# Who scales the probabilities in the mixers' attention heads: VectorE or ScalarE

## The chip, the cores and the metric

The kernel runs on one core of a Trainium2 chip. Its engines are named as in the profile: PE (TensorE, matrix products and transposes), DVE (VectorE), ACT (ScalarE), POOL (GpSimd) and SP (SyncE, which issues the loads). Each has its own queue, carries it out in order and waits for the others by semaphores. The metric is the device time of one execution in microseconds (us), lower is better.

## The reference, cut to what matters

Two transformer blocks run on 256 tokens of width 1024. The second block has two layers. Each begins with a hybrid mixer: a gated delta rule (6 heads), a "forgetting" attention (6 heads) and a pooling branch, whose outputs are concatenated and multiplied by `w_out`. A dense MLP or a mixture of experts follows. The attention is causal, so of the 256x256 scores of a head the block of the first 128 queries has 128 keys, and that of the second has 256:

```python
s = jnp.einsum('bhqd,bhkd->bhqk', q[:, :, lo:hi], k[:, :, :hi]).astype(F32) * scale
s = s + c[:, :, lo:hi, None] - c[:, :, None, :hi]
s = jnp.where(k_pos <= q_pos, s, -jnp.inf)
p = jax.nn.softmax(s, axis=-1).astype(dt)
outs.append(jnp.einsum('bhqk,bhkd->bhqd', p, v[:, :, :hi]))
```

The delta rule needs the inverse of a unit triangular matrix (`triangular_solve` in the reference). The kernel builds it by doubling blocks, in seven levels of which each needs the one before.

## The kernel before, in words

All is float32. A matrix product with weights is done as three products of split numbers: ACT copies a half of a weight tile of 128x2048 into its rounded part (`high`, L1402), DVE subtracts to get the rest (`low`, L1881), PE multiplies (L532 to L534). Three raw tiles (`RING`) and two split ones (`SPLIT`) are in the chip's memory at a time; a split tile is filled again once PE has finished with it.

The order on each engine is written out by hand, once for each engine, in the same steps. In the mixer of layer `l` the six attention heads are interleaved with the levels of the inverse. Step `s` has on each engine:

- PE (`attention`, L627): the scores of head `s`; the transposes of the probabilities of head `s-1` (L646), which wait for `probs`; at odd `s` from 3 the outputs of two heads (L666), which wait for `pt_copied`; then level `s+1` of the inverse (`between_heads`, L1046): twelve products L988, then L997 and L1003 twice. At `s` = 6 there is no level left: `first_chunk` (L1015, `vn0`) stands there, and at `s` = 7 `first_state` (L1041, then L1015 for `o0`), which waits until `vn0` is read.
- DVE (`attention`, L1988): `reciprocal` of the sums of head `s-1` (L1995), the two multiplications by it (L1999, `probs`), the scores of head `s` out of their bank with scale and mask (L2013), their negated row maxima (L2018), then for the inverse `level_mask` (L2354) and the updates (L2405). At `s` = 6 `low(2)` (L1881) stands in the place of the level.
- ACT (`attention`, L1463): first `ahead(s)`, which is the level's copies (`inverse_level`: L1660 `picked` and L1453 `invp`, twice) and at `s` = 6 `high(2)`, four copies of half a weight tile each (L1402); then the exponentials of head `s` (L1459) and the copy of the transposed probabilities of head `s-1` (L1474, `pt_copied`). After step 6 ACT copies out `vn0`, the state and `o0` (L1453).

`PR` holds the scores and then the probabilities of three heads, `RDEN` the reciprocals. The first block's heads (`attention(0, AH)` and `attention(AH, XH)`) use the same functions with `until_now` false.

Of the kernel before, what the change touches and what calls it, by code (L numbers as in the profile page):

```python
# [7 lines left out]
ACT = mybir.ActivationFunctionType  # L8
# [5 lines left out]
TT = S // P  # L14
# [123 lines left out]
def program(nc, A, out, points, stop):  # L138
    ctx = ExitStack()
    with ctx:  # L140
        def sb(name, shape, dt=F32):
            return ctx.enter_context(nc.sbuf_tensor(name, shape, dt))
# [15 lines left out]
        PR = sb("probs", [P, 3, TT, S])  # L158
# [9 lines left out]
        DEN = sb("den", [P, 3, TT])  # L168
        RDEN = sb("rden", [P, 3, TT])
# [110 lines left out]
        def chunk_head(s):  # L280
            return s % 2, s // 2
# [34 lines left out]
        def col(name, i=0):  # L316
            return COL[:, COLS[name] + i:COLS[name] + i + 1]
# [25 lines left out]
        def rows_of(t, until_now):  # L343

            return slice(P * t, P + 2 * P * t) if until_now else slice(S * t, S * t + S)

        def flat(v):
            return v.rearrange("p a b -> p (a b)")
# [23 lines left out]
        def after(*name):  # L372

            key, n = points.get(name, ("pe", 1))
            return sems[key], n
# [139 lines left out]
        with nc.Block() as block:  # L515
# [843 lines left out]
            def _(act):  # L1359
# [19 lines left out]
                def do(ins, *name):  # L1379
                    ins.then_inc(*cact.mark(*name))  # L1380
# [74 lines left out]
                def exps(u, until_now):  # L1455
                    act.wait_ge(*after("negmax", u))
                    for t in range(TT):
                        pr = flat(PR[:, u % 3])[:, rows_of(t, until_now)]
                        do(act.activation(pr, pr, ACT.Exp,  # L1459
                                          bias=NM[:, u % 3, t:t + 1], accum_out=DEN[:, u % 3, t:t + 1]),  # L1460
                           "exp", u, t)

                def attention(u0, heads, between=lambda s: None, until_now=False, ahead=lambda s: None):  # L1463
                    n = P + S if until_now else TT * S
                    for s in range(heads + 1):
                        ahead(s)
                        if s < heads:
                            exps(u0 + s, until_now)
                        if s >= 1:
                            u = u0 + s - 1  # L1470
                            act.wait_ge(*after("pt", u))
                            if u >= 2:
                                act.wait_ge(*after("o", u - 2))
                            do(act.activation(flat(PT[:, u % 2])[:, 0:n], PT_BANK[u % 2][:, 0:n], ACT.Copy),  # L1474
                               "pt_copied", u)
                        between(s)
# [41 lines left out]
                for b in range(4):  # L1518
                    copy_out(QKT[:, 2 * b:2 * b + 2, :], two(psum("qkT", b)), "qkT", b)
                attention(0, AH)  # L1520

                act.wait_ge(*after("read", "cmean"))
# [5 lines left out]
                for i in range(4):  # L1528
                    do(act.activation(C[:, i, :], C[:, i, :], ACT.Silu, bias=col("conv_ln_b", i),
                                      scale=col("conv_ln_g", i)), "csilu")  # L1530
# [9 lines left out]
                def next_query(s):  # L1540
                    if s + 2 < XH:
                        query(s + 2)
                        high(1)

                attention(AH, XH, next_query)
                high(1)
                sum_deferred(3, 3)
# [15 lines left out]
                for l in range(LAYERS):  # L1563
# [66 lines left out]
                    for b in range(3):  # L1630
                        act.wait_ge(*after("filled", "grow", l, b))
                        for c in range(4):
                            t, h = chunk_head(4 * b + c)
# [35 lines left out]
                    def between_heads(s):  # L1669
                        if s + EARLY < LEVELS:  # L1670
                            inverse_level(s + EARLY)
                        if s + EARLY == LEVELS:
                            high(2)

                    attention(AH + XH + NH * l, NH, until_now=True, ahead=between_heads)
                    copy_out(VN[:, 0, :], psum("vn0", l)[:, 0:HW], "vn0", l)
                    copy_out(SST[:, :, :], psum("state", l)[:, 0:3 * HD].rearrange("p (a b) -> p a b", a=3), "state", l)
# [36 lines left out]
                    with act.Fori(0, items) as i:  # L1714
# [62 lines left out]
                        for c in range(2):  # L1777
                            act.wait_ge(*in_loop(i, "pe", "item", f"down{c}"))
                            do(act.activation(YS[:, 0, c, :], item_bank(f"down{c}")[:, :], ACT.Copy,
                                              scale=GSUM[:, 0:1]), "y_high", c)  # L1780
# [77 lines left out]
            def _(dve):  # L1858
                def do(ins, *name):
                    ins.then_inc(*cdve.mark(*name))  # L1860

                def own(back=0):

                    dve.wait_ge(*cdve.last(back))
# [123 lines left out]
                def attention(u0, heads, scale, mask, outs, lag=4, between=lambda s: None, until_now=False):  # L1988


                    for s in range(heads + lag):
                        if 1 <= s <= heads:
                            u = u0 + s - 1
                            dve.wait_ge(*after("exp", u, 1))
                            do(dve.reciprocal(RDEN[:, u % 3, :], DEN[:, u % 3, :]))  # L1995
                            own()
                            for t in range(TT):
                                pr = flat(PR[:, u % 3])[:, rows_of(t, until_now)]
                                do(dve.tensor_scalar(pr, pr, RDEN[:, u % 3, t:t + 1], None, ALU.mult), "probs", u)  # L1999
                        if s < heads:  # L2000
                            u = u0 + s
                            dve.wait_ge(*after("scores", u))
                            if u >= 3:
                                dve.wait_ge(*after("pt", u - 3))
                            ps = SC_BANK[u % 2][:, :]
                            n = P + S if until_now else TT * S
                            pr = flat(PR[:, u % 3])[:, 0:n]
                            if mask is None:
                                for t in range(TT):
                                    do(dve.tensor_scalar(PR[:, u % 3, t, :], ps[:, t * S:(t + 1) * S],  # L2010
                                                         scale[:, t:t + 1], None, ALU.mult), "scores_read", u)
                            else:
                                do(dve.scalar_tensor_tensor(pr, ps[:, 0:n], scale, mask, ALU.mult, ALU.add),  # L2013
                                   "scores_read", u)
                            own()
                            if until_now:
                                for t in range(TT):
                                    do(dve.tensor_reduce(NM[:, u % 3, t:t + 1], pr[:, rows_of(t, True)], AX.X, ALU.max,  # L2018
                                                         negate=True), "negmax", u)
                            else:  # L2020
                                do(dve.tensor_reduce(NM[:, u % 3, :], PR[:, u % 3], AX.X, ALU.max, negate=True),
                                   "negmax", u)
                        if s >= lag:
                            outs(s - lag)
                        between(s)
# [107 lines left out]
                def conv_split():  # L2133
                    dve.wait_ge(*after("csilu"))
                    split(lambda z: CAT[:, z, 4:8, :], C[:, :, :], "convT")

                attention(0, AH, 0.125, flat(logc), outs1)
                conv_mean()
                conv_variance()
# [10 lines left out]
                def outsx(h):  # L2150
                    dve.wait_ge(*after("filled", "xatt_o", h))
                    split(lambda z: CAT[:, z, 2 * h:2 * h + 2, :],
                          psum("xatt_o", h)[:, :].rearrange("p (a b) -> p a b", a=2), "read", "xatt_o", h)

                attention(AH, XH, ns(2, "own"), None, outsx, between=lambda s: low(1) if s in (1, 2) else None)
                sum_deferred(3, "xo")
                for i in range(MLP_SLOTS):
# [28 lines left out]
                for l in range(LAYERS):  # L2186
# [234 lines left out]
                    def between_heads(s):  # L2421
# [10 lines left out]
                        if s + EARLY == LEVELS:  # L2432
                            low(2)

                    attention(AH + XH + NH * l, NH, 0.125, causal, outs2, 2, between_heads, True)

                    def h6(v):
# [302 lines left out]
```

## Time and profile before

| | us |
|---|---|
| median of 3 runs (1479.44 to 1479.93) | 1479.5 |
| profiled execution, its own time | 1477.55 |
| its span, first to last instruction | 1475.7 |
| PE busy | 1396.5 (95%) |
| DVE busy | 1090.0 (74%) |
| ACT busy | 830.9 (56%) |
| mixer heads of layer 0 | 538 to 590 |
| mixer heads of layer 1 | 898 to 950 |

Every time in the rows is counted from the start of the span. "Busy" is a share over stages with different limits, so it doesn't tell what a stage waits for; the chain of waits and the timelines of the stretch do.

### The profile page before, as it was taken

To read this page: it belongs to the slowest core of one execution; us is meant where nothing else is said; L and a number is where in the kernel's file an instruction comes from. 1 tells how busy PE (TensorE), PEld (TensorE's weight loads), DVE (VectorE), ACT (ScalarE), POOL (GpSimd) and SP (SyncE) were. 2 spreads that over 40 slices of the span, in tenths; PEclk is the share of its full clock that TensorE was granted. 3 is DMA by queue.
4 is the path that set the end of the run, shared out by engine and by line. 5 is a ranking of instruction groups with operands and counts; after the bars stand their busy time and mean duration, and the time that the engine had idled before them with its cause. 6 is when DMAs were issued, how large, how long until landed. Compare 5 with 4: busy or idle time off the path is not lost.

```text
span 1475.7 us, 21897 instructions
## 1 busy us (share of the span) xinstructions
PE 1396.5 (95%) x8173; PEld 1221.3 (83%) x8173; DVE 1090.0 (74%) x1583; ACT 830.9 (56%) x1146; POOL 56.1 (4%) x60
## 2 busy tenths in 40 slices
PE   5997899999999999999999999989999999999997
PEld 5795587999988977899999987767888888888886
DVE  4989665656557877655556887677898898898896
ACT  4444454534336754443434483436787787787784
POOL 0000000000002130000000022010000000000000
PEclk9998999999999999999999999987999999999999
DMA  8544052555654510455655440118998998988982
GB/s 301 177 156 154 0 164 88 178 180 191 189 183 136 166 57 15 132 194 176 198 178 177 141 150 30 58 44 303 368 349 308 351 339 298 385 314 306 376 316 111
DMA packets 162964, 292.76 MB, mean 198 GB/s; under 512 B 6832, under 2 KB 78924, under 8 KB 162764
## 3 DMA queue, kind: packets, MB, share of 16 engines
q1 hardware_dynamic: 162336, 291.08, 57.3%
q8 instruction: 50, 0.82, 0.2%
q10 hardware_dynamic: 556, 0.67, 0.1%
q14 instruction: 22, 0.18, 0.0%
HBM read 290.69 MB, written 1.05 MB: 198 GB/s over the span
## 4 chain that ended last, share of the span: by engine, by line
PE 83%; DVE 13%; ACT 2%; issue 1%; DMA 1%; ACTq 0%; SPq 0%; POOL 0%; DVEq 0%
PE bank L532 23%; PE bank L534 23%; PE bank L533 23%; DVE weights_split L1881 4%; DVE arena L2066 3%; PE bank L1176 2%; PE bank L997 1%; PE bank L1249 1%; PE bank L1003 1%; PE bank L988 1%; PE bank L666 1%; PE bank L646 1%; PE bank L1015 1%; PE bank L1226 1%; DMA weights<-in_w_in_dram 1%
## 5 line engine op out<-in xcount | busy, mean ns | idle before, releaser
L1881 DVE TENSOR_TENSOR weights_split<-weights,weights_split 128x1024 fp32r<-128x1024 f32 (+4 forms) x266 | 304.4, 1186 | 172.0 <-ACT weights_split L1402 171.9
L1402 ACT ACTIVATE weights_split<-weights 128x1024 fp32r<-128x1024 f32 (+4 forms) x266 | 258.5, 1022 | 286.0 <-PE bank L534 283.1
L532 PE MATMUL bank<-features_split,weights_split 128*128 128x256 f32 x912 | 262.7, 288 | 15.2 <-DVE features_split L1908 5.4
L533 PE MATMUL bank<-features_split,weights_split 128*128 128x256 f32 x912 | 260.1, 285 | 0.0
L534 PE MATMUL bank<-features_split,weights_split 128*128 128x256 f32 x912 | 260.1, 285 | 0.0
L532 PE MATMUL bank<-weights_split,features_split 128*128 128x512 f32 (+3 forms) x560 | 217.4, 388 | 8.5 <-DVE features_split L1888 3.6
L533 PE MATMUL bank<-weights_split,features_split 128*128 128x512 f32 (+3 forms) x560 | 213.6, 381 | 0.0
L534 PE MATMUL bank<-weights_split,features_split 128*128 128x512 f32 (+3 forms) x560 | 213.5, 381 | 0.0
L532 PEld LDWEIGHTS bank<-features_split,weights_split 128*128 128x128 f32 x912 | 177.2, 194 | 18.9 <-DVE weights_split L1881 6.2
L533 PEld LDWEIGHTS bank<-features_split,weights_split 128*128 128x128 f32 x912 | 177.3, 194 | 0.5
L534 PEld LDWEIGHTS bank<-features_split,weights_split 128*128 128x128 f32 x912 | 177.1, 194 | 0.0
L532 PE MATMUL bank<-weights_split,hidden_split 128*128 128x512 f32 x376 | 148.4, 395 | 1.0 <-DVE weights_split L1881 1.0
L534 PE MATMUL bank<-weights_split,hidden_split 128*128 128x512 f32 x376 | 146.7, 390 | 0.0
L533 PE MATMUL bank<-weights_split,hidden_split 128*128 128x512 f32 x376 | 146.5, 390 | 0.0
L532 PEld LDWEIGHTS bank<-weights_split,features_split 128*128 128x128 f32 x560 | 106.4, 190 | 27.3 <-DVE features_split L1888 4.4
L534 PEld LDWEIGHTS bank<-weights_split,features_split 128*128 128x128 f32 x560 | 106.3, 190 | 17.9
L533 PEld LDWEIGHTS bank<-weights_split,features_split 128*128 128x128 f32 x560 | 106.4, 190 | 16.8
L2654 DVE TENSOR_TENSOR weights_split<-weights,weights_split 128x1024 fp32r<-128x1024 f32 x96 | 115.1, 1222 | 3.9 <-ACT weights_split L1746 2.8
L1746 ACT ACTIVATE weights_split<-weights 128x1024 fp32r<-128x1024 f32 x96 | 100.9, 1058 | 24.2 <-PE bank L534 24.0
L532 PEld LDWEIGHTS bank<-weights_split,hidden_split 128*128 128x128 f32 x376 | 70.7, 188 | 15.6 <-DVE weights_split L1881 2.0
L534 PEld LDWEIGHTS bank<-weights_split,hidden_split 128*128 128x128 f32 x376 | 70.6, 188 | 15.3
L533 PEld LDWEIGHTS bank<-weights_split,hidden_split 128*128 128x128 f32 x376 | 70.7, 188 | 13.8
(364 smaller groups left out, 2261.5 us busy)
## 6 DMA issues: line engine op xcount, KB each, us to landing
weights<-in_moe_gate_dram SPq DMA_DIRECT2D x26, 1024.0 KB, 6.8
weights<-in_moe_up_dram SPq DMA_DIRECT2D x24, 1024.0 KB, 6.8
weights<-in_moe_down_dram SPq DMA_DIRECT2D x24, 1024.0 KB, 7.3
weights<-in_w_in_dram SPq DMA_DIRECT2D x20, 1024.0 KB, 5.2
weights<-in_w_up_dram SPq DMA_DIRECT2D x16, 1024.0 KB, 5.3
weights<-in_w_down_dram SPq DMA_DIRECT2D x16, 1024.0 KB, 4.9
weights<-in_w_out_dram SPq DMA_DIRECT2D x12, 1024.0 KB, 5.0
weights<-in_ffn_gate_dram SPq DMA_DIRECT2D x11, 1024.0 KB, 5.2
```

The costliest lines, as they stand in the source:

```text
L532: pe.matmul(ps, lhs(0), rhs(0), start=start, stop=False, skip_group_check=shared)
L533: pe.matmul(ps, lhs(0), rhs(1), start=False, stop=False, skip_group_check=shared)
L534: return pe.matmul(ps, lhs(1), rhs(0), start=False, stop=stop, skip_group_check=shared)
L646: mm = pe.transpose(ps[:, at:at + P], pr[:, kt * P:(kt + 1) * P], ident)
L666: mm = pe.matmul(ps[o:o + HD, first:S], v[:, kt, h * HD:(h + 1) * HD], flat(pt)[:, kt * S:(kt + 1) * S - first], start=(kt == 0), stop=(kt ...
L988: mm = pe.matmul(inplace(ps[:, i * P:(i + 1) * P].unsqueeze(1), lev), LT[:, p, :], chosen(DI, p, 1, lev), start=True, stop=True)
L1176: mm = pe.matmul(ps[:, k * P:(k + 1) * P], XS[:, z, t, f * P:(f + 1) * P], GSEL[:, t, :], start=(t == 0), stop=(t == TT - 1))
L1402: do(act.activation(split_flat(j)[:, 0, part], raw_flat(j)[:, part], ACT.Copy), "hi", j, b)
L1746: do(act.activation(split_flat(j)[:, 0, part], raw_flat(j)[:, part], ACT.Copy), "hi_item", s, b)
L1881: do(dve.tensor_tensor(split_flat(j)[:, 1, part], raw_flat(j)[:, part], split_flat(j)[:, 0, part].bitcast(F32), ALU.subtract), "lo", j)
L2066: do(dve.scalar_tensor_tensor(C[:, i, :], U[:, i, k:k + S], w, C[:, i, :], ALU.mult, ALU.add), "conv")
L2654: do(dve.tensor_tensor(split_flat(j)[:, 1, part], raw_flat(j)[:, part], split_flat(j)[:, 0, part].bitcast(F32), ALU.subtract), "lo_item", ...
```

## The change

In the mixers' heads alone (`until_now`), the two multiplications by the reciprocal move from DVE to ACT. They become activations with the function Copy and the reciprocal as scale, in place, and stand in ACT's queue at the very start of step `s`, ahead of `ahead(s)`. DVE's reciprocal now has a mark, `rden`, for which ACT waits. The transposes on PE wait for `probs` as before, which ACT now gives. The first block's heads keep theirs on DVE.

```diff
                     for s in range(heads + 1):
+                        if until_now and s >= 1:
+                            u = u0 + s - 1
+                            act.wait_ge(*after("rden", u))
+                            for t in range(TT):
+                                pr = flat(PR[:, u % 3])[:, rows_of(t, True)]
+                                do(act.activation(pr, pr, ACT.Copy, scale=RDEN[:, u % 3, t:t + 1]), "probs", u)
                         ahead(s)
                         if s < heads:
                             exps(u0 + s, until_now)
...
                             dve.wait_ge(*after("exp", u, 1))
-                            do(dve.reciprocal(RDEN[:, u % 3, :], DEN[:, u % 3, :]))
+                            do(dve.reciprocal(RDEN[:, u % 3, :], DEN[:, u % 3, :]), "rden", u)
                             own()
-                            for t in range(TT):
-                                pr = flat(PR[:, u % 3])[:, rows_of(t, until_now)]
+                            for t in range(0 if until_now else TT):
+                                pr = PR[:, u % 3, t, :]
                                 do(dve.tensor_scalar(pr, pr, RDEN[:, u % 3, t:t + 1], None, ALU.mult), "probs", u)
```

The lines behind the change have other numbers in the changed kernel: ACT's L1474, L1660, L1680 and L1683 are L1480, L1666, L1686 and L1689; DVE's L1995, L2013, L2018, L2354 and L2405 are L2001, L2019, L2024, L2360 and L2411.

ACT's queue from the copy of one head's transposed probabilities (`probsT`) to that of the next, steps 1 to 2 of layer 0, before:

```order
L1474 ACTIVATE probsT<-bank 128x384
L1660 ACTIVATE arena<-arena 128x384
L1453 ACTIVATE arena<-bank 128x384
L1660 ACTIVATE arena<-arena 128x384
L1453 ACTIVATE arena<-bank 128x384
L1459 ACTIVATE probs,den<-probs,negmax 128x128
L1459 ACTIVATE probs,den<-probs,negmax 128x256
```

And after:

```order
L1480 ACTIVATE probsT<-bank 128x384
L1471 ACTIVATE probs<-probs,rden 128x128
L1471 ACTIVATE probs<-probs,rden 128x256
L1666 ACTIVATE arena<-arena 128x384
L1453 ACTIVATE arena<-bank 128x384
L1666 ACTIVATE arena<-arena 128x384
L1453 ACTIVATE arena<-bank 128x384
L1459 ACTIVATE probs,den<-probs,negmax 128x128
L1459 ACTIVATE probs,den<-probs,negmax 128x256
```

Two instructions came in ahead of the level's copies; behind them all stands as it was.

ACT's queue at the end of the heads, from `pt_copied` of step 5 over `high(2)` to the copy of `o0`, before:

```order
L1474 ACTIVATE probsT<-bank 128x384
L1402 ACTIVATE weights_split<-weights 128x1024 x4
L1474 ACTIVATE probsT<-bank 128x384
L1453 ACTIVATE arena<-bank 128x384
L1453 ACTIVATE arena<-bank 128x192
L1453 ACTIVATE arena<-bank 128x384
```

And after:

```order
L1480 ACTIVATE probsT<-bank 128x384
L1471 ACTIVATE probs<-probs,rden 128x128
L1471 ACTIVATE probs<-probs,rden 128x256
L1402 ACTIVATE weights_split<-weights 128x1024 x4
L1480 ACTIVATE probsT<-bank 128x384
L1453 ACTIVATE arena<-bank 128x384
L1453 ACTIVATE arena<-bank 128x192
L1453 ACTIVATE arena<-bank 128x384
```

The last head's scaling stands ahead of the four weight copies, and so do the waits that it brings.

DVE's queue over one step (updates, reciprocal, next scores), before:

```order
L2405 TENSOR_TENSOR arena<-arena,bank 128x48x2x4 x4
L1995 RECIPROCAL rden<-den 128x2
L1999 TENSOR_SCALAR probs<-probs,rden 128x128
L1999 TENSOR_SCALAR probs<-probs,rden 128x256
L2013 SCALAR_TENSOR_TENSOR probs<-bank,shape_table 128x384
L2018 TENSOR_REDUCE negmax<-probs 128x1 x2
L2354 TENSOR_TENSOR normed<-normed,shape_table 128x384 x2
```

And after:

```order
L2411 TENSOR_TENSOR arena<-arena,bank 128x48x2x4 x4
L2001 RECIPROCAL rden<-den 128x2
L2019 SCALAR_TENSOR_TENSOR probs<-bank,shape_table 128x384
L2024 TENSOR_REDUCE negmax<-probs 128x1 x2
L2360 TENSOR_TENSOR normed<-normed,shape_table 128x384 x2
```

The two scalings are gone and nothing else moved. PE's queue is the same in both kernels.

## Rows read from the trace of the kernel before

**Rows 1.** The page: the chain that ended last, shares of the span by engine.
```profile
PE 83%; DVE 13%; ACT 2%; issue 1%; DMA 1%; ACTq 0%; SPq 0%; POOL 0%; DVEq 0%
```
**Rows 2.** The chain of waits at layer 0's second head: start us, us, what.
```profile
553.60 1.02 DVE arena L2405 x2
554.62 0.09 DVE rden L1995
...
555.34 0.55 PE bank L646 x3
```
**Rows 3.** DVE's timeline, layer 0: start, us, line, shapes, [idle before, who ended it].
```profile
554.54 0.16 DVE L1995 RECIPROCAL rden<-den 128x2 f32<-128x2 f32 x1
554.73 0.55 DVE L1999 TENSOR_SCALAR probs<-probs,rden 128x128 f32<-128x128 f32 x2
555.21 0.56 DVE L2013 SCALAR_TENSOR_TENSOR probs<-bank,shape_table 128x384 f32<-128x384 f32 x1
...
561.24 0.55 DVE L1999 TENSOR_SCALAR probs<-probs,rden 128x128 f32<-128x128 f32 x2
562.61 0.56 DVE L2013 SCALAR_TENSOR_TENSOR probs<-bank,shape_table 128x384 f32<-128x384 f32 x1 [0.81 <-PE bank L972]
```
**Rows 4.** PE's timeline, layer 0: the third head's transposes.
```profile
562.41 0.49 PE L646 MATMUL bank<-shape_table,probs 128*128 128x128 f32 x3
```
**Rows 5.** ACT's timeline, layer 0: the second head's exponentials, then a level's first copy.
```profile
551.24 0.40 ACT L1459 ACTIVATE probs<-probs,negmax 128x128 f32<-128x128 f32 x1
551.54 0.20 ACT L1459 ACTIVATION_READ_ACCUMULATOR probs<-probs,negmax 128x1 f32 x1
551.63 0.50 ACT L1459 ACTIVATE probs<-probs,negmax 128x256 f32<-128x256 f32 x1
...
556.59 0.49 ACT L1453 ACTIVATE arena<-bank 128x384 f32<-128x384 f32 x1 [2.75 <-PE bank L988]
```
**Rows 6.** Copies on ACT, lines L1654 and L1453: durations min/median/max in ns.
```profile
L1654 ACT ACTIVATE arena<-bank x2: 384/384/385, 539.3 to 897.7; 128x256 f32<-128x256 f32 x2
...
L1453 ACT ACTIVATE arena<-bank,norm_stats x16: 564/586/597, 493.6 to 881.4; 128x384 f32<-128x384 f32 x8, 128x396 f32<-128x396 f32 x4, 128x390 f32<-128x390 f32 x4
```
**Rows 7.** ACT's timeline, the end of layer 0's heads.
```profile
582.54 3.89 ACT L1402 ACTIVATE weights_split<-weights 128x1024 fp32r<-128x1024 f32 x4
586.33 0.49 ACT L1474 ACTIVATE probsT<-bank 128x384 f32<-128x384 f32 x1
586.85 0.49 ACT L1453 ACTIVATE arena<-bank 128x384 f32<-128x384 f32 x1
```
**Rows 8.** The chain of waits there.
```profile
584.27 0.09 DVE rden L1995
...
586.82 0.80 PE bank L666 x6
587.62 0.05 PE bank L1041
```
**Rows 9.** ACT's timeline at the same place of layer 1.
```profile
942.32 3.89 ACT L1402 ACTIVATE weights_split<-weights 128x1024 fp32r<-128x1024 f32 x4
```
**Rows 10.** DVE's timeline at the same place of layer 1.
```profile
943.97 0.16 DVE L1995 RECIPROCAL rden<-den 128x2 f32<-128x2 f32 x1
```
**Rows 11.** PE's waits from 590 to 830, the longest: total, times, longest.
```profile
PE bank L532 <- DVE arena L2495: 1.3, 1, 1.3
```
**Rows 12.** PE in two stretches of layer 1: length, busy (instructions), granted clock, DMA share, GB/s.
```profile
898.00:899.50 1.50, 0.54 (x4) 1.00 0.02 5
...
902.50:904.00 1.50, 1.50 (x9) 0.50 0.00 0
```
**Rows 13.** The chain of waits in layer 1, at the first level.
```profile
902.95 1.28 PE bank L997 x6
904.23 1.21 PE bank L1003 x6
905.44 0.67 PE bank L997 x6
```

## The prediction

> **What bounds the kernel now.** I read the page's chain first: PE holds 83% of it and DVE 13% [rows 1], so a cost or a gain counts where PE stands and waits. Then I read the chain of waits inside the mixers' heads. There PE and DVE take turns: PE ends a level of the inverse, DVE updates the blocks (L2405, two of the four updates on the chain), takes the reciprocal of the head before and scales its probabilities, and PE transposes them (L646) ahead of the next level [rows 2]. Both scalings are on that chain, since PE's queue holds the transposes in front of the next level's products. From the end of the reciprocal to the transposes it is 555.34 - (554.54 + 0.16) = 0.64 us [rows 2, 3]. ACT isn't on the chain there: after the exponentials it stood idle for 2.75 us before the next level's copy out of PSUM [rows 5]. Last I read the end of the heads, where ACT does something large: four copies of half weight tiles, 3.89 us, which in layer 0 began at 582.54, 1.8 us before the last reciprocal ended at 584.27 + 0.09 = 584.36 [rows 7, 8]. Layer 1 is the same picture: copies from 942.32, last reciprocal begun at 943.97 [rows 9, 10].
>
> **DVE's side.** Of 12 heads, 24 scalings go. A pair holds DVE from 554.73 to 555.21, 0.48 us, so 12 x 0.48 = 5.8 us less work [rows 3]. I cost this gain at nothing. What follows on DVE is the scores of the next head, and they are ready only about when the pair is done: at the third head DVE stood 0.81 us for PE's scores after its scaling [rows 3]. Where DVE does begin them earlier, it only gets sooner to `level_mask`, which needs a product that PE makes after the transposes.
>
> **The hand-over in each head.** The reciprocal now goes to ACT by a semaphore, ACT runs two activations, and PE waits for the second. No activation with Copy, a scale per row and 128 or 256 columns from and to this memory is in the trace. The nearest are the exponentials on the same tiles, which also read an operand per row: the next instruction can begin 0.30 us after the 128 wide one, and the 256 wide one lasts 0.50 [rows 5]. A hand-over is 555.34 - (554.73 + 0.55) = 0.06 from DVE to PE [rows 2, 3]; I take the same to ACT. New way: 0.06 + 0.30 + 0.50 + 0.06 = 0.92 us in place of 0.64, so +0.28 a head.
>
> From below: a plain copy of 256 columns without such an operand took 0.38 [rows 6], 0.12 less than the exponential; with that off both, the way is 0.68, +0.04. From above: two copies of 384 columns with the operand, 0.59 each and 0.10 overlapped [rows 5, 6], make 0.06 + 0.49 + 0.59 + 0.06 = 1.20, +0.56. I take the exponentials, since shape and operand are the same. The Trainium skill, "ScalarE: Activation LUTs", section "What ACT_TABLE_LOAD costs", gives an activation with one pointer operand as 280 ns and 0.833 ns a column, whatever the function; for 256 columns that is an estimate of 0.49 us beside the 0.50 of the exponential [rows 5]. No run so far shows it for Copy. The same page, "Rules for kernel authors", sends a multiplication to VectorE and speaks against the change; the 0.55 us of the DVE pair against 0.80 here agrees [rows 3, 5].
>
> Which heads pay: in a layer the first, second, fourth and fifth. The third has cover: DVE scaled from 561.24, ACT would be done at 561.24 + 0.80 + about 0.1 = 562.1, and the transposes began only at 562.41, behind the scores [rows 3, 4, 5]. The cover is thin, 0.3 us, and if it were gone that head would pay up to its 0.28 too. The sixth is counted below. Two layers: 8 x 0.28 = 2.2 us, with ends 0.3 and 4.5.
>
> What is queued behind ACT's new wait in the middle heads are the level's copies. The first of them (`picked`) comes later than before, after the scaling instead of right after the update (by the second update's 0.5, the reciprocal and the 0.8 of the scaling, under 2 us), yet it is needed only with the product's copy, for which ACT idled 2.75 us [rows 5]. I cost it at nothing; without that cover it would be what the pair holds ACT for, 0.30 + 0.40 = 0.7 us a head.
>
> **The end of the heads.** Here the new instructions stand ahead of the weight copies, so these can't start until the last reciprocal is there. The scaling begins at 584.36 + 0.06 = 584.42, its second half at 584.72, and the copies 0.40 later at 585.12 instead of 582.54 [rows 5, 7, 8]. That is +2.58 us for everything behind them on ACT: `pt_copied` of the last head moves from 586.33 to 588.91, and the copy of `vn0` from 586.85 to 589.43, ending 589.92 [rows 7]. PE needs both. The last head's outputs could begin at 588.91 + 0.49 + 0.06 = 589.46 and take half of the pair's 0.80, to 589.86; `first_state` (L1041) waits for `vn0` until 589.98. It began at 587.62 [rows 8]. So PE is late by 589.98 - 587.62 = 2.36 us; this holds the sixth head's own hand-over. The 1.8 us that ACT used to work ahead, while PE and DVE finished the last level, are what is lost, and the scaling on top.
>
> For layer 1 the same rows give the same: ACT's copies begin 943.97 + 0.16 - 942.32 = 1.81 us before the reciprocal's end, against 584.36 - 582.54 = 1.82 [rows 7 to 10]. Both layers: 4.7 us, with ends 4.2 (shorter activations) and 5.3. DVE's subtractions of these tiles wait for the copies too and start over a us later, but PE needs the first tile only behind the state and `o0`; I cost that at nothing.
>
> Does anything behind give it back? Up to 830 PE's longest wait is 1.3 us, for DVE, and that DVE work hangs on PE's own products [rows 11]. No stretch there waits for a transfer which could run on meanwhile. So the delay goes through to the end.
>
> **The sum.** 2.2 + 4.7 = +6.9 us, ends 4.5 and 9.8. Against the profiled execution: 1477.55 + 6.9 = 1484.5. The median shown is 1.95 above that execution's time, so 1479.5 + 6.9 = 1486.4.
>
> **Rivals.**
> - *The clock falls in the new gap.* PE will stand about 0.9 us at the last transposes and again some 2 us before the last outputs, with little work between. In layer 1 the granted clock fell from 1.00 (2.4 GHz) to 0.50 (1.2 GHz) at the first level, after a stretch in which PE was busy for 0.54 of 1.5 us [rows 12]; six L997 and six L1003 took 1.28 and 1.21 us there instead of 0.67 [rows 13], 1.15 us dearer together, and some 1.5 with the products ahead of them. One such fall gives 1486.4 + 1.5 = 1487.9, one in each layer 1489.4. Against it: PE waits for the update and the scaling in every head, and only that one place among the heads shows a fall. The Trainium skill, "TensorE: Matmul & The Clock Gate", Part 1, says that the clock goes by how busy PE has been of late, which by itself is for this rival; the rows show both outcomes. The fall at 902 may also vanish, which is 1.5 less.
> - *The end is covered.* If PE had other work while ACT catches up, only the hand-overs remained: 1479.5 + 2.2 = 1481.7, within what can't be told from no change. For it: L666 and L1041 follow one another without a gap now, so a little slack may be hidden. Against: `first_state` can't be moved past the copy of `vn0`, and the slack of 587.62 against 586.85 + 0.49 = 587.34 is only 0.28 us [rows 7, 8].
> - *DVE was the bound, and the change is faster.* If the levels waited for DVE's queue as a whole and ACT's part were hidden in its idle time, the 5.8 us freed would come off: 1479.5 - 5.8 = 1473.7. It decides where DVE is ready after PE at L2013 or `level_mask`. For it: DVE's two scalings are on the chain [rows 2, 3]. Against: the way over ACT replaces them on that same chain, and DVE waits for PE at L2013 [rows 3].
> - *Another table load on ACT.* Copy between exponentials might need one. Against: before, the level's copies stand between the exponentials already and the second head's begin without a load [rows 5]. I give it nothing.
>
> **Chances.** The forecast 0.60, a fall of the clock 0.28, the end covered 0.08, faster 0.04. Its own bounds make 1484.0 to 1489.3; with one fall of the clock at the upper half and part of the covered case at the lower end I give 1483.2 to 1490.3. What a measurement of this kernel tells from no change is 0.2%, 3.0 us: slower means above 1482.5. The forecast and the clock's case are slower whole, of the covered one about a quarter: slower 0.90, within 0.07, faster 0.03.
>
> **What would show it.** In the changed kernel's profile: L1471 with 0.40 and 0.50 us; L646 about 0.9 us after the reciprocal's end; no idle of DVE less at L2013; L1402 at the heads' end beginning after L1471 and not before; a gap on PE of about 2 us within or before the last L666, ended by ACT; and from there on PE's work later than before by 3.5 us (four hand-overs and the end) in layer 0, 6.9 in layer 1. I'd be wrong if ACT's four copies still ran before the last reciprocal, if L1471 took under 0.2 us, or if the delay at 600 shrank by 830.

## The result, and the profile after

The changed kernel took 1495.82 us in the median of 4 executions (1492.76 to 1497.36), the kernel before 1479.72 beside it: slower, ratio 1.0089 with a 95% interval of 1.0065 to 1.0113. That is 16 us, where 6.9 were forecast. In two later jobs the ratio was 1.0077 (1.0049 to 1.0104) and 1.0083 (1.0057 to 1.0109).

The page of the changed kernel, busy us (share of the span) and instructions, then the chain:

```profile
PE 1408.7 (94%) x8173; PEld 1229.3 (82%) x8173; DVE 1084.6 (73%) x1559; ACT 840.1 (56%) x1170; POOL 56.2 (4%) x60
...
PE 83%; DVE 12%; ACT 3%; issue 1%; DMA 1%; ACTq 0%; SPq 0%; POOL 0%; DVEq 0%
```

DVE lost 24 instructions and ACT got 24. PE has the same 8173, and yet is busy 12 us longer: that is not a wait, it is work that ran slower.

The chain of waits at layer 0's second head, which answers to [rows 2]:

```profile
558.40 0.09 DVE rden L2001
558.50 0.81 ACT probs L1471 x2
559.32 0.04 issue
559.36 0.55 PE bank L646 x3
```

From the reciprocal's end at 558.49 to the transposes it is 0.87 us now, 0.64 before. DVE's timeline there, which answers to [rows 3]:

```profile
558.31 0.16 DVE L2001 RECIPROCAL rden<-den 128x2 f32<-128x2 f32 x1
559.04 0.56 DVE L2019 SCALAR_TENSOR_TENSOR probs<-bank,shape_table 128x384 f32<-128x384 f32 x1 [0.57 <-DVE rden L2001]
```

DVE waits 0.57 us where it used to scale, for scores that are not ready yet (the view names DVE's own reciprocal as the releaser, which had long been done; PE's scores, L970 and L972, ran until 559.0). Its freed time bought nothing. ACT's timeline at the end of layer 0's heads, which answers to [rows 7]:

```profile
590.34 0.80 ACT L1471 ACTIVATE probs<-probs,rden 128x128 f32<-128x128 f32 x2 [1.73 <-DVE rden L2001]
591.04 3.88 ACT L1402 ACTIVATE weights_split<-weights 128x1024 fp32r<-128x1024 f32 x4
```

ACT stands idle for 1.73 us for the last reciprocal, and the weight copies come behind it. The chain of waits over the same stretch, which answers to [rows 8]:

```profile
590.23 0.09 DVE rden L2001
...
591.13 3.79 ACT weights_split L1402 x4
594.92 0.38 ACT probsT L1480
595.30 0.04 issue
595.35 0.69 PE bank L666
...
596.89 0.64 PE bank L1041 x8
597.53 2.75 PE bank L1015 x12
```

The copies are on the chain, as forecast. The last line is the surprise: in the kernel before, the chain has `588.08 1.48 PE bank L1015 x12` for these twelve products. The reason stands in PE's row by stretches (length, busy, granted clock, DMA share, GB/s) of the changed kernel:

```profile
589.50:593.30 3.80, 2.18 (x18) 1.00 0.00 0
593.30:603.50 10.20, 9.02 (x41) 0.50 0.57 208
```

Behind a stretch in which PE was busy for 2.18 of 3.80 us the clock was granted at 0.50, 1.2 GHz, for 10.2 us, and PE was busy for 9.02 of them.

To part the clock from the waits, I compared the start of the same PE instructions in the traces. The table shows by how many us a stretch is longer than in the first trace of the kernel before. "Heads" runs from the first scores to the sixth head's transposes, "end" from there to the transposes L1083 behind the state and `o0`. A star marks a stretch with a fall of the clock that the first trace hasn't (the clock column of each trace's rows). That trace has one of its own in layer 1's heads [rows 13], worth about 1.4; a stretch without it reads that much too low (o). "Behind" goes from the transposes L1083 of layer 1 to 1400 us, and so does the sum. In the last 75 us the falls lie at other places again: by the whole span the five traces are 17.1, 10.4, 14.9, -3.3 and 4.3 longer than the first one of before.

| kernel (trace) | up to the heads | heads 0 | end 0 | heads 1 | end 1 | behind | sum |
|---|---|---|---|---|---|---|---|
| changed, first | 2.20* | 4.00* | 6.06* | -0.17 o | 5.85* | 0 | 17.9 |
| changed, second | 0.02 | 1.15 | 5.95* | 2.68* | 2.28 | -1.6 | 10.4 |
| changed, third | 0.15 | 1.15 | 5.88* | 2.69* | 6.05* | 0 | 15.9 |
| before, second | -0.90* | 0 | 0 | -1.34 o | 0 | 0 | -2.4 |
| before, third | -1.10* | 1.32* | 0 | 1.41* | 3.17* | 0 | 4.8 |

### The profile page after: what moved, and what is told of

It is laid out like the page before. It is cut to its first block, busy times and chain, and to the rows that moved or that the text cites. A ratio compares the mean times of both kernels' runs of the same rounds, so it can differ in the third digit from the quotient of the medians.

```text
span 1492.8 us, 21899 instructions
## 1 busy us (share of the span) xinstructions
PE 1408.7 (94%) x8173; PEld 1229.3 (82%) x8173; DVE 1084.6 (73%) x1559; ACT 840.1 (56%) x1170; POOL 56.2 (4%) x60
## 4 chain that ended last, share of the span: by engine, by line
PE 83%; DVE 12%; ACT 3%; issue 1%; DMA 1%; ACTq 0%; SPq 0%; POOL 0%; DVEq 0%
PE bank L532 23%; PE bank L533 22%; PE bank L534 22%; DVE weights_split L1887 4%; DVE arena L2072 3%; PE bank L1176 2%; PE bank L997 1%; PE bank L1249 1%; PE bank L988 1%; PE bank L1003 1%; PE bank L666 1%; ACT weights_split L1402 1%; PE bank L646 1%; PE bank L1015 1%; PE bank L1226 1%
## 5 line engine op out<-in xcount | busy, mean ns | idle before, releaser
L532 PEld LDWEIGHTS bank<-weights_split,features_split 128*128 128x128 f32 x560 | 107.4, 192 | 27.6 <-DVE features_split L1894 4.4
L534 PEld LDWEIGHTS bank<-weights_split,features_split 128*128 128x128 f32 x560 | 107.4, 192 | 18.4
L533 PEld LDWEIGHTS bank<-weights_split,features_split 128*128 128x128 f32 x560 | 107.6, 192 | 17.2
```

Source lines behind the costliest of these rows:

```text
L532: pe.matmul(ps, lhs(0), rhs(0), start=start, stop=False, skip_group_check=shared)
L533: pe.matmul(ps, lhs(0), rhs(1), start=False, stop=False, skip_group_check=shared)
L534: return pe.matmul(ps, lhs(1), rhs(0), start=False, stop=stop, skip_group_check=shared)
```

## The experiments

The theories: *gap and clock* says that the 16 us are the hand-overs and the late copies, about as forecast, and the rest the lower clock, brought on by the gap that the late copies make on PE. *Phase* or *luck* says that the falls come and go in any kernel with where its work lands in time. The kernel before supplied 115 executions beside these in three jobs: 1473.6 to 1490.8, mean 1479.9 with a standard error of 0.4. So much does one kernel spread; means of many executions are used below beside the medians.

**Heads 1 to 5 alone on ACT (e1_last_dve).**

```diff
-                        if until_now and s >= 1:
+                        if until_now and 1 <= s < heads:
```

DVE scales where ACT doesn't.

> The scaling of heads 1 to 5 of each layer on ACT, that of the sixth on DVE as before, so ACT's weight copies wait for nothing new. Theory 'gap and clock' (the changed kernel's 16 us are 2.2 us of hand-overs, 4.7 us of late ACT copies at the heads' end, some 7 us because TensorE's clock falls to 1.2 GHz in the gap that they make, and a remainder of chance falls): about 2 us over the kernel before, 1481.7, and no fall of the clock at the heads' end. Rival 'phase' (the falls of the clock come wherever the work lands in time, and any small shift brings them): 1482 to 1491, with falls that the kernel before doesn't have.

1485.28 us (10 executions, 1483.92 to 1493.99; ratio 1.0043, 1.0016 to 1.0070), mean 1487.0. The first, second, fourth and fifth heads show the hand-over in the trace, 0.25 us each (0.16 at layer 0's first), and the third nothing; that is the 2 us. But the mean is 7.3 over before's in the same job (1479.7; standard error of the difference 1.5), and this trace has falls behind both ends, of 3.4 us in layer 0 and of 20.5 in layer 1, with the copies not late at all. PE's row of the longer one:

```profile
953.80:974.30 20.50, 20.50 (x91) 0.50 0.28 103
```

"No fall at the heads' end" was wrong, and phase had the better range. The time at half clock (twice one minus the clock, by the span, in the mean of the executions) is 80.5 us against 73.9 of before in this job; 6.6 us more can cost 3.3 at most, so of the 5 us beyond the hand-overs a part stays unexplained. But the falls show that late copies aren't needed for one behind an end.

**The sixth head alone on ACT (e2_last_act).**

```diff
-                        if until_now and s >= 1:
+                        if until_now and s == heads:
```

> Only the sixth head's scaling of each layer on ACT, the others on DVE. Gap and clock: 4.7 us of late copies and 7 us of clock, 1491.5, with some 10 us at 0.50 behind the heads' end in both layers. Phase: 1484.5 and the falls elsewhere, or in one layer alone.

1487.87 us (10; ratio 1.0051, 1.0021 to 1.0081), mean 1487.6. Its trace has the two cases side by side. In layer 0 the clock held, so the late copies stand there by themselves. The chain:

```profile
588.13 0.09 DVE rden L2001
...
589.03 3.79 ACT weights_split L1402 x4
...
593.25 0.64 PE bank L666 x2
...
594.46 1.48 PE bank L1015 x12
```

L1015 takes 1.48, the clock is full; against the first trace the sixth transposes are 0.25 later and L1015 behind the state 2.28 more, 2.53 together. In layer 1 the clock fell for 10.2 us at the same place, and that end is 6.06 longer in place of 2.27: 3.8 us for one fall. Both theories had part: the fall at an end is where gap and clock puts it, but in one layer only, and the heads of both layers have falls (574.7, 936.5) that the first trace hasn't.

**Waiting without scaling (e3_wait_only).** The kernel before, with this ahead of ACT's copies:

```diff
+                        if until_now and s == heads:
+                            u = u0 + s - 1
+                            act.wait_ge(*after("rden", u))
```

> The kernel before, with ACT waiting for the sixth head's reciprocal ahead of its four weight copies and doing nothing else new; all scalings on DVE. By the rows of before the copies then start 584.42 instead of 582.54, 1.9 us late, and PE's first_state about 1.7 us late, twice 1.7 = 3.3 us. Gap and clock: 1483 if this shorter gap keeps the clock, 1490 if it doesn't; the granted clock behind the heads' end must go with the time. Phase: 1483 with or without falls there.

1485.13 us (10; ratio 1.0029, 1.0001 to 1.0056), mean 1484.7. ACT's timeline:

```profile
588.32 3.90 ACT L1402 ACTIVATE weights_split<-weights 128x1024 fp32r<-128x1024 f32 x4 [1.72 <-DVE rden L1998]
```

In layer 0, at full clock, the end is 1.84 us longer, 1.7 reckoned. So 1.84 of the 2.53 of an end is the waiting and 0.7 the scaling ahead of the copies. In layer 1 the clock fell for 3.4 us (953.6 to 957.0) over the sixth head's last outputs and the short wait between them. The mean is 4.9 over before's in this job, where the two ends make 3.7.

**Both gaps filled (e4_fill, e5_fill_short).** The changed kernel, with products on PE whose results nobody reads, ahead of the wait for the sixth head's probabilities and of that for its transposed copy:

```diff
+                            if until_now and s == heads:
+                                for _ in range(FILL0):
+                                    pe.matmul(ps[:, 0:P], ident, ident, start=True, stop=True)
                             pe.wait_ge(*after("probs", u))
...
+                                if until_now and h == heads - 1:
+                                    for _ in range(FILL1):
+                                        pe.matmul(PT_BANK[(u - 1) % 2][:, 0:P], ident, ident, start=True, stop=True)
                                 pe.wait_ge(*after("pt_copied", u))
```

> The changed kernel with 12 products of the unit matrix on PE ahead of its wait for the sixth head's probabilities, and 14 ahead of its wait for that head's transposed copy, which fill the two gaps with work that nobody reads (about 1.3 and 1.6 us at full clock). Gap and clock: the clock stays at 2.4 GHz behind the heads' end and 7 us come back: about 1488 beside the changed kernel's 1495.8, though PE does more work. Phase, or a longer way on ACT than reckoned: 1495 or more.

1490.99 us (10; ratio 1.0081, 1.0056 to 1.0105), mean 1491.0: hardly better than the changed kernel in its other jobs. Yet its trace has no fall in either end. My filling was too long: each product is two instructions of 0.11 us, and by the starts of the same instructions it overran the two gaps of each layer by 0.9 and 1.7 us, 5.1 in all. The sizes were mended:

> The changed kernel with PE's two gaps at the heads' end filled again, now by 6 products of the unit matrix each. In the run with 12 and 14 each product took two passes, 0.22 us, and the filling overran the gaps by 0.9 and 1.7 us a layer; 6 take 1.3 us and fit. Gap and clock: no fall behind the heads' ends and the structural 7 us stay, so 1486, 5 or more below the changed kernel of this job. Luck: the same as the changed kernel within 2 us.

1486.80 us (12 executions, 1484.78 to 1489.59; ratio 1.0042, 1.0020 to 1.0064), mean 1486.8, against a median of 1491.37 and a mean of 1492.0 of the changed kernel in the same job. PE's row by stretches of this kernel; the filling ahead of the sixth head's transposes lies in the first, the other one in the second, and what stands behind the gaps from 592 on:

```profile
584.00:588.00 4.00, 3.76 (x34) 1.00 0.00 0
588.00:592.00 4.00, 3.96 (x31) 1.00 0.02 6
592.00:596.00 4.00, 4.00 (x36) 1.00 0.81 280
```

And its chain:

```profile
589.87 0.80 PE bank L673 x4
590.66 1.53 PE bank L658 x12
592.20 0.64 PE bank L673 x2
...
593.41 1.48 PE bank L1022 x12
```

The filling (L658) ends just as the copy is there, ACT is as late as in the changed kernel (both ends 2.27 us longer), and L1022, the other kernels' L1015, runs at full clock. PE does more work and the kernel is 5.2 us faster in the mean (standard error 1.0), with 70.5 us at half clock in place of 89.4. That shows that these 5 us were the clock, and that PE's idleness around the sixth head brought it down. It doesn't tell which of the two gaps did: the one ahead of the sixth head's transposes was 1.37 us in the kernel before already, the other one is new, and no run fills one alone. What is left over before's mean in this job (1479.6) is 7.2 us, with a standard error of 0.8, the structural part.

**The changed kernel and the kernel before, again (a1_after, b1_before, c3_before, c4_after).**

> The changed kernel unchanged, beside many more executions of the kernel before. The traces so far give, at full clock, 0.25 us a hand-over (8 of them) and 2.5 us for a layer's end: 7 us. Theory 'gap and clock' (the longer gaps bring falls of the clock oftener): the median difference is 12 to 17 us, and the mean granted clock over many executions is lower than before's. Rival 'luck of the first four' (falls come and go alike in both kernels): the difference is 7 us within 2, and the mean clocks agree within 0.001.

1491.37 us (8; 1488.03 to 1497.29). The difference to before's median is 12.7 us. Half-clock time is 89 us in the mean against 73 for the kernel before (43 executions in this job).

> The changed kernel again. The 12 executions so far have a mean of 1493.1, and the 78 of the kernel before one of 1479.4. Gap and clock: mean 1493 within 2, half-clock time longer than before's by some 18 us. If it was luck of few executions, the mean moves toward 1486.

1492.46 us (6; 1491.04 to 1495.00), mean 1492.9. Over all 18 executions the changed kernel has a mean of 1493.1 (standard error 0.6) and 92.5 us at half clock, the kernel before 1479.9 and 72.9. It wasn't the luck of few executions: 13.1 us slower, 19.6 us more at half clock.

> The kernel before against itself, to see how far two sets of its own executions differ and where the clock falls in one more of its traces. Luck: 1479 within 2, and the trace shows falls inside the mixers' heads at places where the first trace had none (around 576, 592 or 953). Gap and clock: 1479 within 2 too, but no fall of over one step (3.4 us) at the heads' end.

1484.59 us (12), mean 1481.5, with the other executions of the same kernel in that job at a median of 1478.69: two sets of 12 and 31 executions of one kernel differ by 6 in the median and 2.6 in the mean. The trace taken was one of the quick ones, without any fall among the heads; what luck expected of it didn't show.

> The kernel before again, for another trace and another set of executions. All theories: mean 1479 within 2. What is open is where the clock falls in an execution near 1485: gap and clock says behind the heads' ends, where a fall of several steps costs 3 to 7 us.

1479.99 us (12), mean 1480.0. This trace has the fall behind an end in the kernel before itself. The chain in layer 1:

```profile
946.37 0.55 PE bank L646 x3
946.92 1.29 PE bank L1015 x12
948.21 1.23 PE bank L666 x6
...
950.28 2.75 PE bank L1015 x12
```

From L666 on PE is at half speed, 3.17 us in all. So the kernel before pays too, at times: one of its six ends (three traces). The changed kernel has it in five of six, for 10.2 us each.

**Sharing the scaling (e6_shared).** ACT takes the 128 wide half of heads 1 to 5, DVE the 256 wide one at the same time:

```diff
-                            for t in range(TT):
...
+                            pr = flat(PR[:, u % 3])[:, rows_of(0, True)]
+                            do(act.activation(pr, pr, ACT.Copy, scale=RDEN[:, u % 3, 0:1]), "probs_first", u)
```

> In heads 1 to 5 of each layer ACT scales only the first 128 rows' probabilities (128 wide) and DVE the others, at the same time; the sixth head stays with DVE. By the traces: from the reciprocal's end 0.04 + 0.40 + 0.04 = 0.48 us instead of 0.64, so 8 x 0.16 = 1.3 us less than before at full clock: 1477.7 if before is 1479. Gap and clock: also fewer falls, if anything. Luck: 1477.7 within the scatter. If the two engines hinder each other on the same tile, 0.64 or more a head and no gain.

1486.87 us (12; 1477.32 to 1491.98; ratio 1.0032, 1.0005 to 1.0060), mean 1485.8. The chain at the first head:

```profile
548.21 0.09 DVE rden L2002
...
548.32 0.46 DVE probs L2006
...
548.82 0.55 PE bank L648 x3
```

PE waits for DVE's half still, which took 0.46 us here where it was 0.36 in the pair before, and a head gains 0.11 us at full clock instead of 0.16. The kernel as a whole is 6 us over before's mean (1479.6 in this job), at 86.6 us of half clock, and its trace has falls behind both ends although nothing is late. I can't explain why this version and e1_last_dve fall there in four ends of four and the kernel before in one of six.

**The kernel before and the shared one, filled (c1_before_fill, c2_shared_fill).** Products as above ahead of the waits for the fifth and sixth heads' probabilities: 4 and 5 in the kernel before, 3 and 5 in the shared one.

```diff
+                            if until_now:
+                                for _ in range(FILLS.get(s, 0)):
+                                    pe.matmul(ps[:, 0:P], ident, ident, start=True, stop=True)
                             pe.wait_ge(*after("probs", u))
```

> The kernel before with 4 products of the unit matrix on PE ahead of its wait for the fifth head's probabilities (gap 1.22 us) and 5 ahead of the sixth's (1.37 us). Its own executions run from 1474 to 1490. Gap and clock: the falls around the fifth and sixth heads go, so the executions near 1485 and above become rare, and the mean of many comes down from 1479.4 to 1476 or 1477, with a higher mean clock. If the falls there depend on more than these two gaps, mean and clock stay as before's.

1484.01 us (12; ratio 1.0018, 1.0002 to 1.0034), mean 1483.6 against 1480.4 of before's 41 executions in this job. The gain didn't come, but the run didn't test what it was made for, since one of the two places was the wrong one. In the trace of the kernel before, the 1.22 us stand ahead of the fourth head's transposes, and at the fifth head the scores fill the wait all but 0.16 us:

```profile
571.35 0.55 PE L646 MATMUL bank<-shape_table,probs 128*128 128x128 f32 x3 [1.22 <-DVE probs L1999]
...
577.87 0.55 PE L646 MATMUL bank<-shape_table,probs 128*128 128x128 f32 x3 [0.16 <-DVE probs L1999]
```

The four products at the fifth head (L644) therefore lie on the chain:

```profile
582.73 0.32 PE bank L976
583.05 0.89 PE bank L644 x8
583.94 0.33 PE bank L650 x3
```

They make each layer 0.55 us longer by the starts of the same instructions, 1.1 of the 3.3 us. The fastest execution is 1480.39 where before has many near 1475. The trace has no fall behind the ends. It has one behind the fourth head's gap in both layers (576.3, 938.1), the gap that wasn't filled, and the clock was no higher on the whole. The fourteen traces have 17 falls between the second and the sixth head's transposes, and each begins there, from 0.5 us ahead of the start of the fourth head's transposes (in the gap) to 1.0 us behind it.

> Heads 1 to 5 with ACT and DVE sharing the scaling (0.11 us a head less at full clock by the last run's trace, about 1 us in all), and the two gaps filled by 3 and 5 products. Gap and clock: 1 us under the kernel before with the same filling, 1475 or 1476 in the mean, and the best of all versions. Otherwise as the shared version without filling, 1486 in the mean.

1481.15 us (12; ratio 1.0004, 0.9987 to 1.0022), mean 1481.3. As fast as the kernel before, not faster, though the three products at the fifth head cost it 0.42 us a layer; 4.5 us under the same version without filling (another job). Four filled kernels give eight ends without a fall. No version tried beats the kernel before.

## Why the prediction was wrong, step by step

- *DVE's side, costed at nothing*: right. DVE waits 0.57 us for the scores in the place of its scaling.
- *The hand-over, +0.28 a head, four heads a layer*: right. It is 0.25 by the starts of the transposes (0.16 at layer 0's first head), and the third head's cover held: its offset is unchanged within 0.01. The nearest rows, the exponentials, gave the activations' times: 0.81 for the pair against 0.80. Eight hand-overs and the sixth heads' two make 1.15 + 1.23 = 2.4 us, by the second changed trace (in layer 1 the 2.68 less 1.45 for a fall, the price that the fifth head shows in e2_last_act).
- *The end of the heads, +2.36 a layer with the sixth's hand-over*: right, measured 0.25 + 2.28 = 2.53 at full clock, in e2_last_act and e5_fill_short. The copies began 0.81 us after the reciprocal, 0.76 reckoned.
- *Nothing gives it back*: right. Between the ends, and from there to 1400 us, the offsets stay within 0.05 us, but for a shorter fall (20.5 us in place of 23.9) in the router's stretch of one trace.
- *The sum*: the terms at full clock are 2.4 + 2 x 2.28 = 7.0 us, forecast 6.9, and the kernel with the gaps filled shows 7.2.
- *The clock*: here it failed. The prediction had the rival, with the right place, at a chance of 0.28 and a price of 1.5 us a fall, and left it out of the sum. Measured, it came in five ends of six and cost 3.6 to 3.8 us each: 6.06, 5.95, 5.88, 6.05 and 5.85 against 2.28. What was mis-sized is the length. The price was taken from one fall of 3.4 us [rows 13], though the same trace has others of 13.7 us (from 137.2) and 23.9 (from 987.2); behind the ends it lasted 10.2. By its length the fall of [rows 13] was even the dearer one, 1.4 for 3.4 us against some 3.7 for 10.2, since PE waits for a part of the latter. Why a fall lasts 3.4 us in one place and 10.2 in another no run shows. In e1_last_dve one lasted 20.5 with PE busy throughout.
- *The gaps*: the argument against that rival, that other waits of the heads brought no fall, was read from one trace. Other traces of the same kernel have falls at such waits (931.4 and 948.4 in c3_before). It also took the wait at the last transposes for 0.9 us, counted from the reciprocal's end; PE stood there for 1.37 us before and for 1.62 after, since DVE's update lies in it too. The second gap was put at some 2 us and is 1.18 in layer 0, where the clock had fallen ahead of it, and 1.53 in layer 1 of a1_after at full clock. Between the two PE does some 3 us of work. The prediction's sign of a gap of about 2 us fits neither alone.

Of the mean of 13.1 us then, 7.0 are structure and 6.1 are clock; at 19.6 us more of half clock that is 0.31 us for each, in line with PE waiting for some of it. How they divide between the late copies and the hand-overs is not shown: heads 1 to 5 alone had 6.6 us more half clock than before in their job (e1_last_dve), the sixth head alone 5.2 (79.1 against 73.9, e2_last_act), and the two together less than the whole change. In the first four executions, which gave the 16, the clock's share was larger: 97 us at half clock against 92.5 over all 18. The trace of the first one also has 2.2 us from falls ahead of the first mixer, where both kernels are the same. That part is chance.

The Trainium skill, "TensorE: Matmul & The Clock Gate", section "HAM oscillation — how this bites in real kernels", tells of a kernel whose waits for DMA bring the lower clock back again and again, so that the work behind a wait pays as well. These traces agree for waits on another engine: 10.2 us at 0.50 behind the gaps of the sixth head, and none with them filled.

What stays open: why e1_last_dve and e6_shared, whose copies aren't late, fall behind the ends in four of four, where the kernel before, with the same 1.37 us at the sixth head, does so in one of six; which of the two gaps counts in the changed kernel; and what filling the fourth head's gap would do in any of them. With one trace each I can't tell whether the places in time or the slightly other gaps in the heads decide. A version shifted in time with its gaps unchanged, which would test phase by itself, wasn't run.

## What to carry to other kernels

Before a step is moved to an idle engine, look at what that engine does ahead of time during the idle stretch: here its four weight copies ran while the others finished, and a wait at the head of its queue took that lead away, which cost more than the step itself. When a change lengthens a gap on PE, put the lower clock into the sum, not as a side case, and price it from all the falls in the trace and not from the shortest. A few products that nobody reads, in the gap and no longer than it, tell how much of a slowdown is clock; read the gap's place from PE's timeline, since at a place without idle time they only cost their length. And where the clock comes and goes, one trace and four executions are a poor measure: compare the starts of the same instructions, stretch by stretch.

## What the runs showed of the hardware

One and the same kernel, before, ran between 1473.6 and 1490.8 us in 115 executions, in clusters near 1475, 1480, 1482 and 1485, and the granted clock went with them (0.979 in the mean of the first, 0.971 in that of the last). The first three executions, within 0.5 us, didn't show it. The falls lie at other times in each trace, also in stretches in which the kernels are the same.
